# First units of a two-layer streaming encoder: weights in blocks of channels, without the norm's factor, and one weight row later

## The reference

```
x  <- x + RMSNorm_post( mixer_i( RMSNorm_pre(x) ) )        i = 0 (mixer A), 1 (mixer B)
A:  [a, g, z] = h W_in            h = RMSNorm_pre(x), W_in 1024 x 3072
    c = a * sigmoid(g)
    y = causal depthwise conv_31(c)
    out = (silu(LayerNorm(y)) * silu(z)) W_out
B:  [u, v] = gelu(h W_uv) ; z = h W_z ; v <- LayerNorm(v)
    s = u * (W_s[group] v + b[group])        per chunk of 128 rows
    out = (s * silu(z)) W_out
```

## Time and profile before

| | us |
|---|---|
| median of 3 runs (lowest, highest) | 2219.44 (2218.34, 2219.84) |
| profiled execution | 2218.88 |
| its span in the profile | 2217.1 |
| PE busy | 2205.6 (99%) |
| DVE busy | 1596.1 (72%) |
| ACT busy | 968.1 (44%) |

### The profile page before, as it was taken

The page is one execution under the profiler, slowest core; times in us unless marked ns, Lnnn a source line. Parts: engine busy times, 40 slices in busy tenths (PEclk is TensorE's granted clock), DMA queues, the critical chain, the costliest instruction groups (busy, mean ns, idle before and its releaser), DMA issues.

```text
span 2217.1 us, 29967 instructions
## 1 busy us (share of the span) xinstructions
PE 2205.6 (99%) x11815; PEld 1942.0 (88%) x11815; DVE 1596.1 (72%) x1990; ACT 968.1 (44%) x1455; POOL 358.1 (16%) x517
## 2 busy tenths in 40 slices
PE   9999999999999999999999999999999999999998
PEld 7888899999888888888888888888889999998887
DVE  6789999997788988999986227852296666667321
ACT  7443333333453225665665125542236656666210
POOL 2111111111221112121110101210112121120000
PEclk9999999999999999999999999999999999999999
DMA  8555666564444313334346426352213333236321
GB/s 302 190 153 153 154 180 189 148 171 120 174 176 162 110 70 110 111 101 125 106 131 217 148 103 221 135 180 88 86 62 93 104 98 107 86 101 241 142 95 38
DMA packets 135436, 303.75 MB, mean 137 GB/s; under 512 B 18176, under 2 KB 54784, under 8 KB 133760
## 3 DMA queue, kind: packets, MB, share of 16 engines
q1 hardware_dynamic: 106192, 203.00, 27.6%
q0 software_dynamic: 28960, 98.57, 15.5%
q10 hardware_dynamic: 144, 0.26, 0.0%
HBM read 223.40 MB, written 78.75 MB: 136 GB/s over the span
## 4 chain that ended last, share of the span: by engine, by line
PE 98%; DMA 1%; DVE 0%; ACT 0%; SPq 0%; issue 0%; POOL 0%; DVEq 0%; POOLq 0%
PE PS L2357 31%; PE PS L2359 31%; PE PS L2358 31%; PE PS L2608 2%; PE PS L2364 1%; PE PS L2363 1%; PE PS L2450 1%; PE PS L2472 1%; DMA rawb<-wb_out_in 0%; DMA B22r<-wb_uz_in 0%; DMA raw<-wa_in_in 0%; PE PS L2459 0%; PE PS L2690 0%; PE PS L2613 0%; DVE S3l L1667 0%
## 5 line engine op out<-in xcount | busy, mean ns | idle before, releaser
L1729 DVE SCALAR_TENSOR_TENSOR acc<-cp,cw,acc 128x513 f32<-128x513 f32 (+3 forms) x464 | 366.9, 791 | 14.3
L2357 PE MATMUL PS<-HAh,Wh 128*128 128x512 f32 (+2 forms) x960 | 340.4, 355 | 3.7 <-DVE HAl L1672 2.2
L2358 PE MATMUL PS<-HAl,Wh 128*128 128x512 f32 (+2 forms) x960 | 338.7, 353 | 0.0
L2359 PE MATMUL PS<-HAh,Wl 128*128 128x512 f32 (+2 forms) x960 | 338.6, 353 | 0.0
L2357 PE MATMUL PS<-Vh,HBh 128*128 128x512 f32 x512 | 199.6, 390 | 0.0
L2359 PE MATMUL PS<-Vh,HBl 128*128 128x512 f32 x512 | 199.2, 389 | 0.0
L2358 PE MATMUL PS<-Vl,HBh 128*128 128x512 f32 x512 | 199.2, 389 | 0.0
L2357 PEld LDWEIGHTS PS<-HAh,Wh 128*128 128x128 f32 x960 | 180.4, 188 | 20.1 <-DVE Wl L1667 4.2
L2357 PE MATMUL PS<-Wbh,s7h 128*128 128x512 f32 x500 | 195.3, 391 | 0.0
L1756 DVE SCALAR_TENSOR_TENSOR over<-pair,cg,over 128x512 f32<-128x512 f32 (+1 forms) x240 | 189.9, 791 | 7.4
L2359 PE MATMUL PS<-Wbh,s7l 128*128 128x512 f32 x500 | 194.6, 389 | 0.0
(11 more groups left out here) (255 smaller groups left out, 5227.0 us busy)
## 6 DMA issues: line engine op xcount, KB each, us to landing
raw<-wa_in_in SPq DMA_DIRECT2D x48, 512.0 KB, 4.7
Wl<-wa_in_in POOLq DMA_DIRECT2D x39, 512.0 KB, 5.7
rawv<-wb_v_in SPq DMA_DIRECT2D x64, 256.0 KB, 5.0
QWr<-wb_uz_in SPq DMA_DIRECT2D x64, 256.0 KB, 2.6
v_scratch<-vb POOLq DMA_DIRECT2D x64, 256.0 KB, 2.6
vt<-v_scratch SPq DMA_DIRECT2D x32, 512.0 KB, 3.9
s_scratch<-m POOLq DMA_DIRECT2D x32, 512.0 KB, 4.0
rawb<-wb_out_in SPq DMA_DIRECT2D x28, 512.0 KB, 8.3
```

What stands on the lines that cost most here:

```text
L1729: return nc.vector.scalar_tensor_tensor(out=out, in0=src, scalar=w, in1=first, op0=ALU.mult, op1=ALU.add)
L2357: nc.tensor.matmul(out, wh, xh, start=start, stop=False, skip_group_check=seeded)
L2358: nc.tensor.matmul(out, wh, xl, start=False, stop=False, skip_group_check=seeded)
L2359: return nc.tensor.matmul(out, wl, xh, start=False, stop=stop, skip_group_check=seeded)
```

## The change

Four things are changed, of which the first three belong together:

1. *First units.* Weights of units 0 to 2 come from a second copy `wa_first`, in blocks: block k holds the 128 input channels k of all three units (192 KB). Their tiles (`firstr`, `firsth`) lie over the slots' room until both chunks are done. PE takes block k of all three units at once: three products high by high, three with low input, three with low weight, each three behind its own wait.
2. *The norm's factor.* Chunk 1 of these units is also made without it. DVE multiplies it in (`first_factor`, `first_gate` for a second chunk too), sigmoid and silu then work in place on `cs` and `zc`; x is normalised for both chunks only for unit 3 and on, both from `xg`.
3. *Orders.* `a_order` goes (3,0) (4,0) (5,0) (3,1) (4,1) (5,1); before (3,1) (4,1) (3,0) (4,0) (5,0) (5,1). Weights of 6 and 7 are split at (4,0) and (5,1); before, those of 5 and 6 at (3,1) and (4,0). Rows are squared in the order of t; the transposes come in five groups, before in nine. The first `c_load` stands in SP's queue behind the load of unit 6, before it stood ahead of it.
4. *End.* In the second half, row 3's products with high weights stand behind the low ones of rows 1 and 2.

```diff
+KEEP = 3
 FIRST = ((0, 0), (1, 0), (2, 0), (0, 1), (1, 1), (2, 1))
-FIRST_ROWS = [(0, k) for k in range(3)] + [(1, k) for k in range(3)] + [(0, 3), (1, 3)] + [(2, k) for k in range(4)]
-FIRST_ROWS += [(n, k) for k in range(4, KD) for n in range(3)]
-X_ORDER = (4, 5, 6, 7, 0, 1, 2, 3) + tuple(range(8, 17))
-AHEAD_A = {(3, 1): 5, (4, 0): 6}
+SECOND_ROWS = [(n, k) for k in range(KH) for n in range(3)] + [(n, k) for n in range(3) for k in range(KH, KD)]
+AHEAD_A = {(4, 0): 6, (5, 1): 7}
...
-        a_order = list(FIRST) + [(3, 1), (4, 1), (3, 0), (4, 0)]
-        a_order += [(n, c) for n in range(5, 2 * UNITS_A) for c in range(NCH[n // UNITS_A])]
+        a_order = list(FIRST) + [(n, c) for c in range(2) for n in range(3, 6)]
+        a_order += [(n, c) for n in range(6, 2 * UNITS_A) for c in range(NCH[n // UNITS_A])]
...
-                    sp.dma_start(HAr[0][:, k, CW:], x_t0[k, :, CW:]).then_inc(n1_ldk[k], 16)
+                    sp.wait_ge(a_hi, k + 1)
+                    sp.dma_start(xg[1][:, k, :], x_t0[k, :, CW:]).then_inc(n1_ldk[k], 16)
...
+            def first_load(k):
+                sp.dma_start(firstr[:, :, 1, k * P:(k + 1) * P], wa_first[k, :, :, :]).then_inc(n1_ldk[k], 16)
...
-            a_load(0)
             x_row(0, 0)
-            sp.dma_start(par[:, :], chan_par).then_inc(ld_con, 16)
+            sp.dma_start(par[:, :], chan_par).then_inc(ld_filters, 16)
+            first_load(0)
+            for k in range(1, KD):
+                x_row(k, 0)
+                first_load(k)
             sp.dma_start(con[:, :], consts).then_inc(ld_con, 16)
-            x_row(1, 0)
-            x_row(2, 0)
-            a_load(1)
-            x_row(3, 0)
-            a_load(2)
-            for k in range(4, KD):
-                x_row(k, 0)
+            x_load(0)
...
+            x_row(0, 1)
...
+            x_row(1, 1)
...
+            for k in range(2, KD):
+                x_row(k, 1)
+            a_load(3)
             for t in range(4, 8):
...
-            for k in range(KD):
-                x_row(k, 1)
-            for t in range(4):
-                x_load(t)
-            a_load(3)
...
+            def first_weight_high(k):
+                act.wait_ge(n1_ldk[k], 32)
+                ks = slice(k * P, (k + 1) * P)
+                nc.scalar.activation(firsth[:, :, 0, ks], firstr[:, :, 1, ks], ACT.Copy).then_inc(a_hi, 1)
+
...
-                if 6 <= p < 9:
-                    n1_square(8 + p)
+                if 6 <= p < 11:
+                    for t in range(2 * p - 4, min(2 * p - 2, NTILES)):
+                        n1_square(t)
...
+            def first_sigmoid(c):
+                half = cs[:, c * CW:(c + 1) * CW]
+                act.wait_ge(a_norm, 3 * c + 1)
+                nc.scalar.activation(half, half, ACT.Sigmoid).then_inc(a_sig, 1)
+
+            def first_silu(c):
+                half = zc[:, c * CW:(c + 1) * CW]
+                act.wait_ge(a_norm, 3 * c + 3)
+                nc.scalar.activation(half, half, ACT.Silu).then_inc(a_zs, 1)
+
+            for k in range(KD):
+                first_weight_high(k)
+                first_high(k, 0)
+            n1_square(0)
+            n1_square(1)
+            first_high(0, 1)
+            n1_square(2)
+            first_high(1, 1)
+            n1_square(3)
+            for k in range(2, KD):
+                first_high(k, 1)
+            n1_factors(0)
+            first_sigmoid(0)
+            n1_high(0, 0)
+            n1_square(4)
+            n1_high(1, 0)
+            n1_high(2, 0)
+            n1_square(5)
+            n1_high(3, 0)
+            a_high(3)
+            n1_high(4, 0)
+            n1_square(6)
+            n1_high(5, 0)
+            n1_high(6, 0)
+            n1_square(7)
+            a_high(4)
+            n1_high(7, 0)
+            a_high(5)
+            n1_factors(1)
+            first_silu(0)
+            first_sigmoid(1)
             for k in range(KD):
                 n1_high(k, 1)
-                if k in (1, 3, 5, 6):
-                    n1_square((1, 3, 5, 6).index(k))
-            n1_factors(0)
-            a_high(3)
-            act.wait_ge(a_norm, 1)
-            nc.scalar.activation(cs[:, 0:CW], cs[:, 0:CW], ACT.Sigmoid).then_inc(a_sig, 1)
-            for k in range(2):
-                n1_high(k, 0)
-            a_gate(0, 1)
-            n1_high(2, 0)
-            a_high(4)
-            n1_high(3, 0)
-            n1_square(8)
-            n1_square(9)
-            act.wait_ge(a_norm, 3)
-            nc.scalar.activation(zc[:, 0:CW], zc[:, 0:CW], ACT.Silu).then_inc(a_zs, 1)
-            a_gate(2, 1)
-            for k in range(4, KD):
-                n1_high(k, 0)
-                n1_square(k + 6)
+            first_silu(1)
...
+            def first_weight_low(k):
+                dve.wait_ge(a_hi, k + 1)
+                ks = slice(k * P, (k + 1) * P)
+                split_low(firsth[:, :, 1, ks], firstr[:, :, 1, ks], firsth[:, :, 0, ks], a_lo)
...
                 if c == 1:
                     if k == 0:
-                        dve.wait_ge(n1_tr, 4)
-                    dve.wait_ge(n1_ldk[k], 32)
-                    out = src = HAr[0][:, k, CW:]
-                    factors = PS[:, 7, :]
+                        dve.wait_ge(n1_row, 2)
+                        dve.wait_ge(a_mm, 6)
+                    out, src, factors = HAr[0][:, k, CW:], xg[1][:, k, :], rnc[:, CW:]
...
-            def first_factor(n, count):
-
+            def first_factor(n, c):
+
+                cols = slice(c * CW, (c + 1) * CW)
                 out = cs if n == 0 else zc
-                dve.wait_ge(n1_row, 1)
-                dve.wait_ge(a_mm, n + 1)
-                nc.vector.tensor_tensor(out[:, 0:CW], PS[:, n, 0:CW], rnc[:, :], ALU.mult).then_inc(a_norm, count)
+                dve.wait_ge(n1_row, c + 1)
+                dve.wait_ge(a_mm, 3 * c + n + 1)
+                nc.vector.tensor_tensor(out[:, cols], PS[:, 3 * c + n, 0:CW], rnc[:, cols], ALU.mult).then_inc(a_norm, 1)
...
+            def first_gate(c):
+                cols = slice(c * CW, (c + 1) * CW)
+                dve.wait_ge(a_sig, c + 1)
+                nc.vector.tensor_tensor(cs[:, cols], cs[:, cols], rnc[:, cols], ALU.mult).then_inc(a_norm, 1)
...
-            a_low(0)
-            first_low(0)
-            first_low(1)
-            first_low(2)
-            a_low(1)
-            first_low(3)
-            a_low(2)
-            for k in range(4, KD):
-                first_low(k)
+            for k in range(KD):
+                first_low(k, 0)
+                first_weight_low(k)
...
+            for k in range(KD):
+                first_low(k, 1)
+            first_factor(0, 0)
+            n1_scale(0, 0)
+            for k in range(1, KD):
+                n1_scale(k, 0)
+                n1_low(k - 1, 0)
+                if k == 4:
+                    a_low(3)
+                if k == 5:
+                    first_gate(0)
+                if k == 6:
+                    dve.wait_ge(a_norm, 2)
+                    a_product(1, 0)
+            n1_low(KD - 1, 0)
+            a_low(4)
+            first_factor(2, 0)
+            a_low(5)
+            first_factor(0, 1)
             n1_scale(0, 1)
             for k in range(1, KD):
                 n1_scale(k, 1)
                 n1_low(k - 1, 1)
+                if k == 4:
+                    first_gate(1)
             n1_low(KD - 1, 1)
-            first_factor(0, 1)
-            n1_scale(0, 0)
-            n1_scale(1, 0)
-            a_low(3)
-            n1_low(0, 0)
-            n1_scale(2, 0)
-            dve.wait_ge(a_sig, 1)
-            nc.vector.tensor_tensor(cs[:, 0:CW], cs[:, 0:CW], rnc[:, :], ALU.mult).then_inc(a_norm, 1)
-            n1_low(1, 0)
-            dve.wait_ge(a_norm, 2)
-            a_product(1, 0)
-            n1_scale(3, 0)
+            dve.wait_ge(a_norm, 5)
             a_product(1, 1)
-            n1_low(2, 0)
-            a_low(4)
             first_factor(2, 1)
-            n1_scale(4, 0)
-            n1_low(3, 0)
-            for k in range(5, KD):
-                n1_scale(k, 0)
-                n1_low(k - 1, 0)
-            n1_low(KD - 1, 0)
...
-                for i, (n, k) in enumerate(FIRST_ROWS):
-                    if k == 0:
-                        pe.wait_ge(a_lo, n + 1)
+                for k in range(KD):
+                    pe.wait_ge(a_hi, k + 1)
+                    pe.wait_ge(n1_hi, k + 1)
+                    for n in range(KEEP):
+                        nc.tensor.matmul(PS[:, n, :], first_weights(n, k)[0], HAh[0][:, k, 0:CW], start=k == 0, stop=False)
                     pe.wait_ge(n1_lo, k + 1)
-                    last = a_row(n, 0, k)
+                    for n in range(KEEP):
+                        nc.tensor.matmul(PS[:, n, :], first_weights(n, k)[0], HAl[0][:, k, 0:CW], start=False, stop=False)
+                    pe.wait_ge(a_lo, k + 1)
+                    for n in range(KEEP):
```

(38 more changed lines are left out.)

159 lines of the change are left out of this document (76 added, 83 removed).

## The result

| | before | after |
|---|---|---|
| median (lowest, highest), us | 2219.11 (2218.34, 2219.84), 6 runs | 2229.57 (2228.19, 2231.18), 6 runs |
| ratio, 95% interval | | 1.0047 [1.0034, 1.006] |
| span of the profiled execution | 2217.1 | 2227.8 |

The changed kernel is 10.5 us slower. I had said 2222.5, in 2218.0 to 2226.0: the sign and the mechanism of the likeliest case, but a third of the size, and outside the range.

What follows compares the result with a forecast made beforehand. DVE, without slack up to the O stage, was taken to bound the kernel: profiled 2218.88 + 3.1 for DVE's lateness + 0 for the late row = 2222.0, with the median 0.56 above 2222.5; range 2218.0 to 2226.0.

Steps and rivals of the forecast that it cites:

- the likeliest case: Whole kernel: DVE leaves the start late and hands this on to the end; 2222.5 us, chance 0.5.
- What bounds the kernel: Convolution to O stage: PE is busy 99%, but DVE has no slack, so its lateness reaches PE at 518.
- low 8: DVE's low weights of unit 8, last station of the start's walk: to end at 89.2 against 86.1 before.
- PE's start: First units on PE: first product at 5.95, 48 rows over at 39.2, a lead of 4.7 us (4.1 to 5.2).
- DVE leaves the start 3.1 us late: DVE up to unit 8's low weights: ends at 89.2 against 86.1; bounds +1.3 to +6.
- issue 39.2: Unit 5's weight load: issued at 39.2, once PE is done with both chunks of units 0 to 2.
- 4.9 to landing (the median is 5.0): Unit 5's weight load: lands 4.9 us after its issue, at 44.1.
- back by 63.2: Product (1,1) on DVE at 59.9, POOL stores at once, and the load back is issued by 63.2.
- Rival C: Longer chain behind unit 5, from late landings, ACT's queue or PE's clock: 4.5 to 8 us, 2224 to 2227.5; chance 0.3.
- rival B: PE's lead from the start survives to the end: 2214.6 us, with the late row 2213.9; chance 0.1.
- Where PE's lead goes: PE's waits up to 518: 2 us at unit 14, 4 at unit 17, 2 at the statistics.
- The late row: Row 3 near 2025 us: 0.6 to 0.8 gained is given back at 2033; 0, with -0.8 as the end.

Runs made afterwards that it cites:

- dve_delay: Kernel before with four useless products of about 1.25 us each put on DVE at chunk (18, 0): 2226.19 us, ratio 1.0035.
- x_after_w5: Changed kernel with two tiles of x moved from ahead of unit 5's load to behind it in SP's queue: 2225.21 us, ratio 1.0031.
- the three rebuilt ones: Changed kernel with x tiles behind unit 5's load, unit 4's convolution steps earlier, ACT reordered; then fewer early squares; then later x loads: 2222.14, 2221.51, 2216.02 us.
- taps_only: Changed kernel with the first load back ahead of unit 6's load and unit 4's convolution steps ahead of unit 6's low weights: 2227.71 us, ratio 1.0042.
- late_spreads: Changed kernel with the last three groups of transposes one chunk later and ACT's factor copies one or two chunks later: 2227.57 us, ratio 1.0042.
- late_product: Kernel before with only DVE's product of (1,1) moved behind the last split of normalised x: 2219.23 us, ratio 1.0004.

## Why the prediction was wrong, point by point

**What bounds the kernel: right.** In all rows but dve_delay, which sets the delay behind low 8 on purpose, the statistics stand off from before by what low 8 does (0.5 at most between them), and the end is off from the statistics by at most 1.3. PE's lead at the start was worth nothing in the changed kernel.

**PE's start: 5.98 as said, its lead too large.** The 0.03 is luck: in the nine kernels with this start the first product comes between 5.98 and 7.02. The first blocks of loads didn't keep pace: ACT waited 1.34 and 1.54 us for the second and third, and chunk 1 began 1.2 later than summed. That is near the 1.4 that I had worked out for slower blocks and not taken. At the end of the 48 rows the lead was 3.4, outside 4.1 to 5.2.

**The step that failed: "DVE leaves the start 3.1 us late".** It left 11.4 late. The walk is right in its stations and wrong in three of its terms. Low 8 was to end at 89.2; it ended at 97.5, 8.3 later, and 6.5 of that are these three:
- "issue 39.2": unit 5's load was issued at 40.97 (+1.8, PE's smaller lead).
- "4.9 to landing (the median is 5.0)": it took 6.76 (+1.9). A median of loads with other neighbours was the wrong row; in the kernel before unit 5's own load took 3.80. Two tiles of x, issued 1.8 to 2.3 us ahead of it, are still in flight, and so is unit 4's load. In the changed kernel and the four others that keep this order of the queue it took 5.5 to 7.0; with the tiles behind it (x_after_w5 and the three rebuilt ones) 3.6 to 4.5.

```profile
38.25 0.33 SPq L699 DMA_DIRECT2D raw<-wa_in_in  x1
38.67 0.86 SPq L678 DMA_DIRECT2D xq<-x_in  x2
40.97 0.33 SPq L699 DMA_DIRECT2D raw<-wa_in_in  x1
```

- "back by 63.2", a store of 3.3: it took 6.12 (+2.8), the largest of the three. The 3.27 of the earlier trace rows is a store with no load beside it. By making the product late, the change puts the store beside unit 6's load; taps_only shows 3.16 without that load.

The rest, 1.8, is in small pieces: 0.4 up to the product, 0.4 until POOL issues the store, 0.3 on ACT, and 0.8 between low 6 and low 8, of which 0.57 is the wait for unit 8's weights, held by the second store, and 0.2 one for a gate.

The upper end of my bounds had such landings ("landing in 7", "a store of 4.3"), but its +6 was too low, since a store of 6 and a load issued 1.8 late weren't thought of. Rival C had the right condition (unit 5's high weights end after 46.5; they ended at 48.8) and too low a top, 2227.5. Two slips in the sums change nothing: 448 KB in 2.05 us are 224 GB/s, not 219, and rival B takes off 4.8 where the lead was 4.7.

**Where PE's lead goes: wrong in place.** 2 at unit 14, 4 at unit 17, 2 at the statistics were said. It was 7.4 in one wait at 97 us, on the factors that stand on ACT behind the second store, and 1.6 for the statistics. The sum didn't depend on it, as said: late_spreads took that wait away, and its end stayed with DVE's lateness (+9.0 at the statistics, +7.9 at the end).

**The clock.** Rival C had asked what a wait of 4 us does. The windows of the changed kernel show the granted clock fall within the wait of 7.4 and come back once PE works again:

```profile
88.00:92.00 4.00, 1.55 (x7) 0.94 (x5) 3.93 (x5) 0.00 (x0) 0.00 (x0) 1.00 1.01 345
92.00:97.00 5.00, 0.02 (x1) 0.05 (x1) 4.25 (x7) 3.48 (x5) 0.00 (x0) 0.65 1.00 398
97.00:101.00 4.00, 4.00 (x11) 3.13 (x12) 3.86 (x6) 2.92 (x5) 0.86 (x1) 0.58 0.05 22
101.00:104.00 3.00, 3.00 (x15) 2.47 (x14) 2.86 (x5) 0.00 (x0) 0.10 (x1) 1.00 0.74 115
```

It cost nothing at the end here, since PE still came early enough to wait 1.6 us for the statistics; behind that wait of 1.6 the clock stayed full. In dve_delay, where the wait of 4.2 was at the hand-over itself, it cost 1.5. (By the Trainium skill, "TensorE: Matmul & The Clock Gate", Part 1, an idle PE is clocked down; the traces agree: 1.00 ahead of these two waits, 0.58 and 0.57 behind them.)

**The late row: right.** 0.

**Small loads.** The Trainium skill's advice of 1 MiB a DMA ("DMA: Bandwidth & Descriptors", "Bandwidth") points the right way at the start, by 1.2 us and not 1.6; but no run cut the loads in another way, so that their size, and not SP's issues (0.6 us each, two a block) or the other loads, was the cause isn't shown.

**The last 0.7.** Of the 11.5 us at the statistics 10.7 are left at the end. Most of the difference belongs to the kernel before, at one place. There DVE waits 3.02 us for a load, and PE then waits 0.27 for DVE:

```profile
852.39 0.69 DVE L2022 TENSOR_TENSOR QWr<-B22r,B12r 128x512 f32<-128x512 f32 x1 [3.02 <-DMA B22r<-wb_uz_in]
...
856.26 0.50 PE L2357 MATMUL PS<-HBh,QW 128*128 128x512 f32 x1 [0.27 <-DVE QW L1667]
```

In the changed kernel that load took 7.0 us and not 7.9, DVE comes 0.8 sooner, PE doesn't wait, and PE's lateness falls from 11.5 to 11.0 at this product. late_product loses the same 0.5 there. The rest goes in small steps that I can't name.
